# A decoder layer in fp32r matmuls: the stationary tiles of hT, the combinations and aT hold their two token blocks interleaved

## The reference

```
h = rms_norm(x, attn_norm_g)
proj = h @ w_in
merged = sigmoid(g_da) * (o_da @ w_o_da) + sigmoid(g_ret) * (o_ret @ w_o_ret) + sigmoid(g_mem) * (o_mem @ w_o_mem)
x = x + merged @ w_out
hf = rms_norm(x, ffn_norm_g)
x = x + (silu(hf @ w_ffn_gate) * (hf @ w_ffn_up)) @ w_ffn_down
```

## Time and profile before

| | |
|---|---|
| runs | 1628.01 and 1627.34 us, median 1627.67 us |
| span of the profiled execution, first to last instruction | 1625.4 us |
| around the span, median less span | 2.3 us |
| granted TensorE clock | 1.000 over the span |
| PE busy | 1618.2 us of 7373 matmuls |
| weight loads busy | 1339.3 us |
| DVE busy | 1271.1 us (78%) |
| ACT busy | 908.2 us (56%) |
| HBM | 197 GB/s over the span |

### The profile page before, as it was taken

The page is one execution under the profiler, slowest core; times in us unless marked ns, Lnnn a source line. Parts: engine busy times, 40 slices in busy tenths (PEclk is TensorE's granted clock), DMA queues, the critical chain, the costliest instruction groups (busy, mean ns, idle before and its releaser), DMA issues.

```text
span 1625.4 us, 20227 instructions
## 1 busy us (share of the span) xinstructions
PE 1618.2 (100%) x7373; PEld 1339.3 (82%) x7373; DVE 1271.1 (78%) x1325; ACT 908.2 (56%) x989; POOL 80.6 (5%) x73
## 2 busy tenths in 40 slices
PE   9999999999999999999999999999999999999999
PEld 7888888888888888888888888888888888888887
DVE  5565545589777777777975589999999999999995
ACT  6654454555555554445554465656655665656653
POOL 0000000000011100000000000100100100100101
PEclk9999999999999999999999999999999999999999
DMA  9876555556554555566675756868868868868866
GB/s 339 278 214 194 157 180 175 174 179 220 179 166 162 164 172 168 174 188 199 202 245 182 249 166 207 252 211 248 246 212 250 249 208 249 244 220 240 253 211 178
DMA packets 178007, 341.35 MB, mean 210 GB/s; under 512 B 11793, under 2 KB 16401, under 8 KB 177169
## 3 DMA queue, kind: packets, MB, share of 16 engines
q1 hardware_dynamic: 167056, 319.45, 60.4%
q0 software_dynamic: 10880, 20.97, 7.1%
HBM read 317.31 MB, written 2.10 MB: 197 GB/s over the span
## 4 chain that ended last, share of the span: by engine, by line
PE 90%; issue 6%; DVE 1%; DMA 1%; POOL 1%; ACT 1%; SPq 0%; DVEq 0%; ACTq 0%; POOLq 0%
PE acc L1582 43%; PE at L1664 9%; PE at L1666 9%; PE at L1665 9%; PE acc L1666 5%; PE acc L1664 5%; PE acc L1665 5%; PE at L1582 3%; PE at L1604 2%; POOL rstd L480 1%; PE at L1642 0%; PE at L1657 0%; DMA raw<-in_w_mem_kv 0%; DMA raw<-in_w_in 0%; DVE w_lo L929 0%
## 5 line engine op out<-in xcount | busy, mean ns | idle before, releaser
L929 DVE TENSOR_TENSOR w_lo<-raw,w_hi 128x1024 fp32r<-128x1024 f32 x319 | 386.6, 1222 | 239.6 <-ACT w_hi L507 235.4
L507 ACT ACTIVATE w_hi<-raw 128x1024 fp32r<-128x1024 f32 x319 | 337.1, 1060 | 360.9 <-PE acc L1582 300.3
L1582 PE MATMUL acc<-w_hi,hT_hi 128*128 128x512 f32 x752 | 297.6, 396 | 0.0
L1582 PE MATMUL acc<-w_hi,hT_lo 128*128 128x512 f32 x752 | 293.1, 390 | 0.0
L1582 PE MATMUL acc<-w_lo,hT_hi 128*128 128x512 f32 x752 | 293.0, 390 | 0.0
L857 ACT ACTIVATE f_hi<-sum 128x2048 fp32r<-128x2048 f32 x60 | 115.3, 1922 | 121.2 <-DVE sum L1461 118.0
L1582 PEld LDWEIGHTS acc<-w_hi,hT_hi 128*128 128x128 f32 x752 | 141.2, 188 | 30.9 <-issue 1.3
L1582 PEld LDWEIGHTS acc<-w_hi,hT_lo 128*128 128x128 f32 x752 | 141.2, 188 | 29.7
L1582 PEld LDWEIGHTS acc<-w_lo,hT_hi 128*128 128x128 f32 x752 | 141.3, 188 | 28.4
L1582 PE MATMUL acc<-w_hi,oT_hi 128*128 128x512 f32 x384 | 151.2, 394 | 1.5 <-DVE oT_lo L955 1.4
L1582 PE MATMUL acc<-w_hi,oT_lo 128*128 128x512 f32 x384 | 149.6, 390 | 0.0
(11 more groups left out here) (349 smaller groups left out, 2658.1 us busy)
## 6 DMA issues: line engine op xcount, KB each, us to landing
raw<-in_w_in SPq DMA_DIRECT2D x208, 512.0 KB, 3.8
f_raw<-in_w_ffn_down SPq DMA_DIRECT2D x88, 512.0 KB, 4.8
f_raw<-in_w_ffn_gate SPq DMA_DIRECT2D x80, 512.0 KB, 3.9
f_raw<-in_w_ffn_up SPq DMA_DIRECT2D x80, 512.0 KB, 5.0
proj<-down POOLq DMA_DIRECT2D x40, 512.0 KB, 6.4
raw<-in_w_mem_kv SPq DMA_DIRECT2D x32, 512.0 KB, 6.2
raw<-in_w_out SPq DMA_DIRECT2D x32, 512.0 KB, 3.7
raw<-in_w_o_mem SPq DMA_DIRECT2D x16, 512.0 KB, 5.0
```

What stands on the lines that cost most here:

```text
L507: act.activation(w_hi[:, s % RING], raw[:, s % RING], ACT.Copy).then_inc(hi_done, 1)
L929: v.tensor_tensor(w_lo[:, s % RING], raw[:, s % RING], w_hi[:, s % RING].bitcast(F32), ALU.subtract).then_inc(lo_done, 1)
L1582: e = pe.matmul(dst, a[:, k0 + k, tok], w[:, s % RING, k, :], start=first and k == 0 and n == 0, stop=last and k == 1 and n == 2)
```

## The change

Every stationary tile of hT, of the combinations and of aT is stored with its two token blocks interleaved word by word. Tile t of hT and aT becomes words t, t + 2, t + 4 and so on of a row block of 256; combinations c = 0 and 1 share one block of 256 words, 2 and 3 another. A load of 128 stationary columns then reads every other word of 1024 bytes instead of 512 bytes in a row. The moving side, the products, their order, all waits and all semaphores stay. oT stays as it was, and so do the tiles of the attention parts. To write the new layout:

- `x_t` is permuted on the host, so that hT is filled interleaved by the same loads and the same instructions;
- the transposes of `turn_columns` and `turn_acts` write their 128 columns to every other word of PSUM, and ACT and DVE copy them on in a row as before;
- the DVE instructions that make the combinations read and write every other word;
- the slices that PE loads are stepped.

```
-            def three_passes(...):   tok = slice(t * P, (t + 1) * P)
+                tok = slice(t, TOK, TB) if hi is hT_hi else slice(t * P, (t + 1) * P)
...
-                return hT_hi[:, k, t * P:(t + 1) * P], hT_lo[:, k, t * P:(t + 1) * P]
+                return hT_hi[:, k, t::TB], hT_lo[:, k, t::TB]
...
-                        e = turn(at[:, k % 4, t * P:(t + 1) * P], src[:, t, c0 + k * P:c0 + (k + 1) * P])
+                        e = turn(at[:, k % 4, t:TOK:TB], src[:, t, c0 + k * P:c0 + (k + 1) * P])
...
-                        c0 = (k % 2) * 256 + t * P
-                        e = turn(dst[:, k // 2, c0:c0 + P], gt[:, t, k * P:(k + 1) * P])
+                        c0 = (k % 2) * TOK
+                        e = turn(dst[:, k // 2, c0 + t:c0 + TOK:TB], gt[:, t, k * P:(k + 1) * P])
...
-                return cmb_hi[:, i, c, :] if i < 4 else cmb_hi4[:, i - 4, c, :], cmb_lo[:, i, c, :]
+                hi = cmb_hi[:, i] if i < 4 else cmb_hi4[:, i - 4]
+                return hi[:, c // 2, :, c % 2], cmb_lo[:, i, c // 2, :, c % 2]
...
-                    e = product(at[:, 2 * (n % 2) + t, :], hi[:, k, t * P:(t + 1) * P],
-                                lo[:, k, t * P:(t + 1) * P], *whole(f, p, u, k), k == 0, k == 3)
+                    e = product(at[:, 2 * (n % 2) + t, :], hi[:, k, t::TB], lo[:, k, t::TB], *whole(f, p, u, k),
+                                k == 0, k == 3)
...
-                a11, a12 = pairs[:, :, 0, 0:P], pairs[:, :, 1, 0:P]
-                a21, a22 = pairs[:, :, 0, P:2 * P], pairs[:, :, 1, P:2 * P]
-                v.tensor_tensor(mixed[:, :, 3], a11, a21, ALU.subtract).then_inc(done, 1)
+                a11, a12, a21, a22 = (pairs[:, :, k, t::TB] for t in range(TB) for k in range(2))
+                v.tensor_tensor(mixed[:, :, 1, :, 1], a11, a21, ALU.subtract).then_inc(done, 1)
...
-        "x_t": inputs["x"][0].T, "mem_t": inputs["mem"][0].T,
+        "x_t": inputs["x"][0].T.reshape(D, TB, P).transpose(0, 2, 1).reshape(D, TOK), "mem_t": inputs["mem"][0].T,
```

More of the change, by code:

```diff
@@ L161, in program @@
                     for t in range(TB):
-                        for name, shape, dt in (("r_cmb", [P, 4, 4, P], F32R), ("r_sum", [P, 4, NCOL], F32R if stage else F32),
+                        for name, shape, dt in (("r_cmb", [P, 4, 2, P, 2], F32R), ("r_sum", [P, 4, NCOL], F32R if stage else F32),
                                                 ("r_hi", [P, 4, NCOL], F32R), ("r_act", [P, 2 * NCOL], F32)):
@@ L182, in program @@
             ("rows_t0", rows_tile, F32), ("f_raw2", quad_tile, F32), ("sum0", quad_tile, F32), ("act_t0", act_tile, F32),
-            ("rows_t1", rows_tile, F32), ("sum1", quad_tile, F32), ("cmb_hi", [P, 4, 4, P], F32R),
+            ("rows_t1", rows_tile, F32), ("sum1", quad_tile, F32), ("cmb_hi", [P, 4, 2, P, 2], F32R),
             ("act_t1", act_tile, F32),
-            ("cmb_lo", [P, NS, 4, P], F32R), ("cmb_hi4", [P, 2, 4, P], F32R))
+            ("cmb_lo", [P, NS, 2, P, 2], F32R), ("cmb_hi4", [P, 2, 2, P, 2], F32R))
         with ExitStack() as ffn:
@@ L226, in program @@
         p_whole = p_sum[1][:, 0, :].rearrange("p (k c) -> p k c", k=2)
[L227 removed]
+        p_mixed = p_sum[1][:, 1, :].rearrange("p (a m b) -> p a m b", a=2, b=2)
         p_out = [[proj[:, :, (2 * r + c + 8) * NCOL:(2 * r + c + 9) * NCOL] for c in range(2)] for r in range(2)]
@@ L825, in _ @@
                     act.wait_ge(cmb_f, 5)
-                    act.activation(cmb_hi[:], sums[1][:].rearrange("p q (c m) -> p q c m", c=4),
+                    act.activation(cmb_hi[:], sums[1][:].rearrange("p q (a m b) -> p q a m b", a=2, b=2),
                                    ACT.Copy).then_inc(cmb_split, 1)
@@ L829, in _ @@
                     act.wait_ge(cmb_f4, 5)
-                    act.activation(cmb_hi4[:], sums[0][:, 2:4].rearrange("p q (c m) -> p q c m", c=4),
+                    act.activation(cmb_hi4[:], sums[0][:, 2:4].rearrange("p q (a m b) -> p q a m b", a=2, b=2),
                                    ACT.Copy).then_inc(cmb_split, 1)
@@ L1054, in _ @@
                     if s == 2:
[L1055 to L1058, removed]
+                        a11, a12, a21, a22 = (p_whole[:, k, t::TB] for t in range(TB) for k in range(2))
+                        v.tensor_tensor(p_mixed[:, 1, :, 1], a11, a21, ALU.subtract).then_inc(p_cmb, 1)
+                        step(v.tensor_tensor(p_mixed[:, 0, :, 0], a22, a21, ALU.subtract), p_cmb, i * 5 + 3)
+                        step(v.scalar_tensor_tensor(out=p_mixed[:, 0, :, 1], in0=p_mixed[:, 0, :, 0], scalar=-1.0, in1=a11,
                                                     op0=ALU.mult, op1=ALU.subtract), p_cmb, i * 5 + 4)
-                        v.tensor_tensor(p_mixed[:, 2], a12, p_mixed[:, 1], ALU.add).then_inc(p_cmb, 1)
+                        v.tensor_tensor(p_mixed[:, 1, :, 0], a12, p_mixed[:, 0, :, 1], ALU.add).then_inc(p_cmb, 1)
                     if s == 8:
@@ L1297, in _ @@
                     if s == 2:
[L1298 to L1301, removed]
+                        a11, a12, a21, a22 = (r_whole[:, k, t::TB] for t in range(TB) for k in range(2))
+                        v.tensor_tensor(r_mixed[:, 1, :, 1], a11, a21, ALU.subtract).then_inc(r_cmb, 1)
+                        step(v.tensor_tensor(r_mixed[:, 0, :, 0], a22, a21, ALU.subtract), r_cmb, i * 5 + 3)
+                        step(v.scalar_tensor_tensor(out=r_mixed[:, 0, :, 1], in0=r_mixed[:, 0, :, 0], scalar=-1.0, in1=a11,
                                                     op0=ALU.mult, op1=ALU.subtract), r_cmb, i * 5 + 4)
-                        v.tensor_tensor(r_mixed[:, 2], a12, r_mixed[:, 1], ALU.add).then_inc(r_cmb, 1)
+                        v.tensor_tensor(r_mixed[:, 1, :, 0], a12, r_mixed[:, 0, :, 1], ALU.add).then_inc(r_cmb, 1)
                     if s == 6:
@@ L1410, in combine @@
                                      hT_lo[:, 2 * q0:2 * q1, :].bitcast(F32), ALU.add), done, 1)
-                a11, a12 = pairs[:, :, 0, 0:P], pairs[:, :, 1, 0:P]
-                a21, a22 = pairs[:, :, 0, P:2 * P], pairs[:, :, 1, P:2 * P]
-                v.tensor_tensor(mixed[:, :, 3], a11, a21, ALU.subtract).then_inc(done, 1)
-                step(v.tensor_tensor(mixed[:, :, 0], a22, a21, ALU.subtract), done, 3)
-                step(v.scalar_tensor_tensor(out=mixed[:, :, 1], in0=mixed[:, :, 0], scalar=-1.0, in1=a11, op0=ALU.mult,
+                a11, a12, a21, a22 = (pairs[:, :, k, t::TB] for t in range(TB) for k in range(2))
+                v.tensor_tensor(mixed[:, :, 1, :, 1], a11, a21, ALU.subtract).then_inc(done, 1)
+                step(v.tensor_tensor(mixed[:, :, 0, :, 0], a22, a21, ALU.subtract), done, 3)
+                step(v.scalar_tensor_tensor(out=mixed[:, :, 0, :, 1], in0=mixed[:, :, 0, :, 0], scalar=-1.0, in1=a11, op0=ALU.mult,
                                             op1=ALU.subtract), done, 4)
-                step(v.tensor_tensor(mixed[:, :, 2], a12, mixed[:, :, 1], ALU.add), done, 5)
-            mixed4 = sums[1][:].rearrange("p q (c m) -> p q c m", c=4)
+                step(v.tensor_tensor(mixed[:, :, 1, :, 0], a12, mixed[:, :, 0, :, 1], ALU.add), done, 5)
+            mixed4 = sums[1][:].rearrange("p q (a m b) -> p q a m b", a=2, b=2)
             last = sums[0][:, 0:2].rearrange("p q (k c) -> p q k c", k=2)
-            mixed1 = sums[0][:, 2:4].rearrange("p q (c m) -> p q c m", c=4)
+            mixed1 = sums[0][:, 2:4].rearrange("p q (a m b) -> p q a m b", a=2, b=2)
             def low_whole(f, p, u):
@@ L1692, in combined @@
                 def combined(c):
-                    return p_cmb_hi[:, i, c, :], p_cmb_lo[:, i, c, :]
+                    return p_cmb_hi[:, i, c // 2, :, c % 2], p_cmb_lo[:, i, c // 2, :, c % 2]
                 pe.wait_ge(lo_done, g + 2)
@@ L1822, in combined @@
                 def combined(c):
-                    return r_cmb_hi[:, i, c, :], r_cmb_lo[:, i, c, :]
+                    return r_cmb_hi[:, i, c // 2, :, c % 2], r_cmb_lo[:, i, c // 2, :, c % 2]
                 pe.wait_ge(lo_done, g + 2)
```

7 lines of the change are left out of this document (3 added, 4 removed).

## The result

The changed kernel takes 1660.54 us (median of two runs, 1659.64 to 1661.43) against 1627.67: a ratio of 1.0202, 95% interval 1.0173 to 1.0232. It is slower by about 2% (the interval leaves open on which side of 2% it lies), where 3.4% faster was forecast.

The account below looks back on a forecast made before the run. PE's own pace was taken to bound the kernel; 1625.4 us of span less 28.6 (before 977 us) and 26.5 (feed-forward stage) gives 1570.3, forecast 1573 us (-3.4%) with the time around it, range 1560 to 1660.

Parts of the forecast that it names:

- The bound and the count: Whole kernel: PE's own pace sets the time; 5445 matmuls are touched, 2649 before 977 us and 2796 after.
- the load with a step of two words: PE loads of hT, combinations and aT: 10.8 ns less per matmul, saving 28.6 us before 977 us and 26.5 after.
- in step with the fp32r stream: Touched PE matmuls: stepped load and stream both move 9.6 bytes a ns, so pace becomes 215.9 ns; chance 0.53.
- The contrast that it rested on: Memory attention's fp32 scores take 216 ns at half the stream's pace, fp32r matmuls 227: 10.8 ns less with the same load.
- The floor of 32 cycles that I wanted to remove: Each fp32r matmul pays 13.4 ns above the pure stream; at best all of it goes, 73 us over 5445 matmuls.
- The rival on the slower side: Matmuls loading hT, combinations or aT slow to 237.5 ns: 59 us more, 1687 us (+3.6%); chance 0.20.
- by the memory that it touches: Under each load, 1024 touched bytes instead of 512 take 21.6 ns of reading from the stream instead of 10.8.
- The rival of no change: PE loads cost the same at either step, the extra belonging to full-pace fp32r: 1628 us, up to 1641; chance 0.27.
- The rule that the load has a port of its own: PE loads take nothing from the stream, speaking for no change; it implies equal pace for scores and hT.
- The terms taken at nothing: PSUM transposes, DVE combinations, permuted x_t: 0 us; bounds 13 us for transposes, 9 and 4.5 us for combinations if doubled.
- The rule on PSUM patterns: Non-contiguous PSUM patterns slow matmuls significantly; the 120 transposes would cost up to 13 us more.
- The feed-forward's limit by DVE: Feed-forward: PE would save 28.1 us, but DVE can come forward only 24.4 us, so 24.4 is counted.

Follow-up runs that it names:

- experiment 2: Kernel of PE work alone, layer left out, varying column counts, types and stream steps against the first bare load-pattern kernel; 384 columns took 173 ns at load steps 1 and 2.

## Why the prediction was wrong

**The bound and the count were right.** PE's own pace is the only thing that moved, no wait appeared, and 5445 touched matmuls times the difference of pace give 34 us, where some 33 came.

**The step that failed is the value taken for the load with a step of two words**, "in step with the fp32r stream", at the pace of the fp32 scores, 215.9 ns. The runs show 233.3. The contrast that it rested on was real: fp32 at half the stream's pace doesn't pay, and bf16 doesn't either. But I read it as two readers at unequal speeds that meet again and again, and let equal speeds be free. Neither half of this holds. The speeds would not have been equal: 512 bytes in 0.11 us are 4.65 bytes a ns and not 4.8, and at step 2 the load has a pace of 118 ns, 8.7 bytes a ns against the stream's 9.6. And at two to one, the step of the kernel before, the pace already runs from 226.7 to 234.3 ns with the start word, so it is the position and not the ratio of speeds that costs. The layer's loads at step 1 stood at the best position found and those at step 2 at a bad one (0.2333, where 0.2300 was the best of their step). The floor of 32 cycles that I wanted to remove was in every fp32r pace measured with 512 columns, at any step and start word.

**The rival on the slower side** had the sign, and its price was too high: 10.8 ns a matmul was expected, 6.7 came, hardly above the 6 ns from which it decides. Its mechanism, "by the memory that it touches", is refuted: a load of 128 words in a row costs the same 6.7 ns when it starts at word 8.

**The rival of no change** by the rule of 16-byte lines was right about the load itself (111 and 118 ns when alone, 233 at step 4) and wrong about the time, because the stream pays. The rule that the load has a port of its own and takes nothing from the stream (the Trainium skill, TensorE: Matmul & The Clock Gate, Part 2) doesn't hold for an fp32r stream here: 32 bytes of padding between the two change the pace from 226.7 to 233 ns.

**The terms taken at nothing held**: transposes into every other PSUM word, DVE's stepped combinations, the permuted x_t; together 1.000 (0.9991 to 1.001). The rule on PSUM patterns (the Trainium skill, Advanced Engine Details and Errata, PSUM Cachelines), which had up to 13 us, doesn't show at the pace of these fp32 transposes, 0.11 us each in either layout. The feed-forward's limit by DVE was never put to the test, since PE didn't become faster.

**What stays open.** That the difference of address and the line before decide is shown; which part of the memory the two readers contend for, if they do, is not, nor why the floor is 32 cycles, nor whether it needs a load. A pattern that beats the kernel before was looked for at step 1 in eighteen start words up to 60, at step 2 in twelve, and none went below 226.7 ns. The order of different patterns, which also counts, was tried for a few pairs only. Tiles that all lie at multiples of 64 words, as in the kernel before, are at the best pace found, so these runs gave no candidate for a faster layer.

## What to carry to other kernels

When TensorE streams fp32r at full pace, the pace depends on where the stationary tile lies against the moving one: read start-to-start times, not matmul lengths, and for 512 columns keep both at multiples of 64 words (256 bytes) with loads of words in a row, 226.7 ns, where other start words take up to 234.3. For other column counts measure again: at 448 the same position paid 48 cycles. Small paddings between tiles are then no detail, and a layout change has to be tried with its addresses. A contrast between two rows that differ in type, pace and pattern at once can't carry a forecast; one kernel of bare matmuls would have given this price before the layout was touched.

## What the runs showed of the hardware

- Where the stream is short (128 columns of fp32r), a load of 128 words sets a pace of 111 ns at step 1, 118 at step 2 and 233 at step 4. With 512 columns step 4 costs only 2 ns more than step 2 (235 against 233), though the load alone now needs the whole pace.
- An fp32r stream that itself reads every other word takes (669.00 - 611.08) / 128 = 0.452 us for 512 columns (experiment 2), twice the time of words in a row, where a bf16 stream at step 2 goes from 216 to 226.
- The same pair of load and matmul from the same addresses takes 226.7 or 233.3 ns, depending on the line that ran before it.
- After two lines of 128-column matmuls, 111 and 118 ns apart, the granted clock fell from 2.4 to 1.2 GHz, though PE never stood idle, and it rose again among the first fp32 matmuls of 256 columns (experiment 2). The pace of 233 ns that the load sets was the same at either level.
- 32 bytes of padding in each partition cost 1.3% of a kernel of 1.6 ms.
